# Two stacks of gated layers on one core: the order of work at the edges of the stages, and the token sums moved from GpSimd to VectorE

## The reference

```python
for l in range(2):                                   # first block
    x = x + 0.5 * swiglu(rmsnorm(x, ffn1_norm[l]), gate, up, down)    # ffn1_l
    h = rmsnorm(x, mix_norm[l])                                       # mix_l
    x = x + concat(sliding_window, moba, top_k_sparse)(h @ w_in[l]) @ w_out[l]
    x = x + 0.5 * swiglu(rmsnorm(x, ffn2_norm[l]), gate, up, down)    # ffn2_l
x = rmsnorm(x, final_norm)                                            # final
h = h + rms_norm(diff_attention(rms_norm(h)))        # second block: diff
h = h + rms_norm(conv_ffn(rms_norm(h)))              # conv_0
h = h + rms_norm(forgetting_attention(rms_norm(h)))  # fox
h = h + rms_norm(conv_ffn(rms_norm(h)))              # conv_1
```

## Time and profile before

| | us |
|---|---|
| median of 3 runs | 3137.25 (3136.92 to 3137.4) |
| the profiled execution | 3136.89 |
| its span in the trace | 3135.1 |
| PE busy | 3085.1 (98%) |
| DVE busy | 2095.1 (67%) |
| ACT busy | 1372.0 (44%) |
| POOL busy | 821.9 (26%) |
| granted clock of PE, mean | 0.998 of full speed |

### The profile page before, as it was taken

The page is one execution under the profiler, slowest core; times in us unless marked ns, Lnnn a source line. Parts: engine busy times, 40 slices in busy tenths (PEclk is TensorE's granted clock), DMA queues, the critical chain, the costliest instruction groups (busy, mean ns, idle before and its releaser), DMA issues.

```text
span 3135.1 us, 47847 instructions
## 1 busy us (share of the span) xinstructions
PE 3085.1 (98%) x17664; PEld 2608.0 (83%) x17664; DVE 2095.1 (67%) x3335; ACT 1372.0 (44%) x2308; POOL 821.9 (26%) x627
## 2 busy tenths in 40 slices
PE   8999999999999999999999999999999999999999
PEld 6999876898989899777899977677888886778887
DVE  6869587685958586695867753556556546576474
ACT  5535246452535353354634433644334335343242
POOL 3212346521333133264412220240000332310003
PEclk9999999999999999999999999999999999999999
DMA  4355331333334433221343333123333231223232
GB/s 125 106 148 153 102 101 41 94 102 101 104 85 115 114 88 102 77 61 54 101 121 89 103 93 96 39 61 87 107 87 100 81 96 41 68 68 109 86 99 82
DMA packets 530032, 289.14 MB, mean 92 GB/s; under 512 B 13630, under 2 KB 520225, under 8 KB 529850
## 3 DMA queue, kind: packets, MB, share of 16 engines
q1 hardware_dynamic: 527162, 281.26, 31.4%
q0 software_dynamic: 2688, 5.44, 0.5%
HBM read 284.38 MB, written 10.02 MB: 94 GB/s over the span
## 4 chain that ended last, share of the span: by engine, by line
PE 84%; DVE 7%; issue 3%; ACT 3%; POOL 1%; SPq 1%; DMA 0%; DVEq 0%; ACTq 0%; POOLq 0%
PE bank L2373 38%; PE bank L2426 24%; PE bank L2391 5%; PE bank L2679 3%; PE bank L2789 2%; PE bank L2408 2%; PE bank L2476 2%; PE bank L2831 2%; PE bank L2854 1%; PE bank L2611 1%; PE bank L2517 1%; ACT w_hi L1009 1%; DVE w_lo L1612 1%; DVE h_lo L1642 1%; DVE scaled_g L1725 0%
## 5 line engine op out<-in xcount | busy, mean ns | idle before, releaser
L1009 ACT ACTIVATE w_hi<-w_raw 128x1024 fp32r<-128x1024 f32 (+1 forms) x319 | 367.6, 1152 | 1003.4 <-PE bank L2373 612.0
L1612 DVE TENSOR_TENSOR w_lo<-w_raw,w_hi 128x1024 fp32r<-128x1024 f32 (+2 forms) x287 | 420.1, 1464 | 254.8 <-ACT w_hi L1009 254.7
L2373 PE MATMUL bank<-h_hi,w_hi 128*128 128x512 f32 (+1 forms) x1204 | 476.7, 396 | 11.5 <-DVE h_lo L1642 4.5
L2373 PE MATMUL bank<-h_hi,w_lo 128*128 128x512 f32 (+1 forms) x1204 | 469.3, 390 | 0.0
L2373 PE MATMUL bank<-h_lo,w_hi 128*128 128x512 f32 (+1 forms) x1192 | 464.8, 390 | 0.0
L2426 PE MATMUL bank<-h_hi,ws 128*128 128x256 f32 x2432 | 452.7, 283 | 0.4 <-DVE ws L1796 0.4
L2426 PEld LDWEIGHTS bank<-h_hi,ws 128*128 128x128 f32 x2432 | 385.9, 192 | 1.4 <-DVE ws L1796 0.8
L2426 PE MATMUL bank<-h_lo,ws 128*128 128x256 f32 x1216 | 344.1, 283 | 0.0
L2426 PE MATMUL bank<-t_hi,ws 128*128 128x256 f32 x1824 | 341.1, 283 | 0.0
L2373 PE MATMUL bank<-act_hi,w_hi 128*128 128x512 f32 x836 | 325.3, 389 | 0.0
L2373 PE MATMUL bank<-act_hi,w_lo 128*128 128x512 f32 x836 | 325.2, 389 | 0.0
(11 more groups left out here) (390 smaller groups left out, 6245.6 us busy)
## 6 DMA issues: line engine op xcount, KB each, us to landing
w_raw<-in_ffn_w_down_dram SPq DMA_DIRECT2D x64, 704.0 KB, 4.7
w_raw<-in_ffn_w_in_dram SPq DMA_DIRECT2D x88, 512.0 KB, 3.8
raw_g<-in_ffn_w_gate_dram SPq DMA_DIRECT2D x76, 512.0 KB, 3.9
raw_u<-in_ffn_w_up_dram SPq DMA_DIRECT2D x67, 512.0 KB, 3.8
w_raw<-in_ffn_w_out_dram SPq DMA_DIRECT2D x32, 704.0 KB, 4.6
w_raw<-in_w_in_dram SPq DMA_DIRECT2D x34, 512.0 KB, 3.8
w_raw<-in_a_w_qkv_dram SPq DMA_DIRECT2D x24, 512.0 KB, 3.8
w_raw<-in_w_out_dram SPq DMA_DIRECT2D x16, 512.0 KB, 3.9
```

Source lines behind the costliest of these rows:

```text
L1009: nc.scalar.activation(split_home(c)[0][:, 0:nk, 0:cols], raw[c % 2][:, 0:nk, 0:cols], ACT.Copy).then_inc(hi_ready, 1)
L1612: nc.vector.tensor_tensor(w_low[:, 0:nk, 0:cols], raw[c % 2][:, 0:nk, 0:cols], w_high[:, 0:nk, 0:cols].bitcast(f32), ALU.subtract).then_in ...
L2373: mm = nc.tensor.matmul(result(c)[0:cols, :], w[:, k, 0:cols], x[k], start=(k == 0 and n == 0), stop=(k == nk - 1 and n == 2))
```

## The change

SP loads unit 3 and the first fast pair's up columns ahead of the four `lam_in` tables, and ACT makes `hi(3)` ahead of the first block of `full_input`. The four token sums are made by DVE (`token_sum(name, n)`): in the first gated stage around the first pairs' work, in the other three the first two before `invert` and the last two behind `lo(c + 3)`; POOL no longer makes them. In the first gated stage `gate_whole(1)` comes before `product_whole(0)`. `output_gemm` with a following stage makes the last `take` before `h_low` 5, 6 and 7. POOL's `pair_scale` makes the low part of the unit between the first phase's scaling and the second's. ACT's `finish` makes `hi(c + 2)` behind its loops. In the convolution stages `lead` is 3 for the first half, ACT's `hi(at + 2)` does not wait for the gate bank, and in the third pair DVE makes `lo(at + 2)` before it empties the gate bank.

```diff
--- before.py
+++ after.py
@@ -677,10 +677,8 @@
             def fast_ff(name, gate, up, down):
 
                 c = BASE[name]
-                for u in range(3 if c == 0 else 0, 2 * FAST_FROM[0]):
+                for u in range(4 if c == 0 else 0, 2 * FAST_FROM[0]):
                     load(c + u, (gate, up)[u % 2][:, :, P * (u // 2):P * (u // 2 + 1)])
-                    if c == 0 and u == 3:
-                        fast_up(name, 0, FAST_FROM[0], up)
                 for j in range(FAST_FROM[0], FH):
                     fast_gate(name, 0, j, gate)
                     if c or j > FAST_FROM[0]:
@@ -745,6 +743,8 @@
                           A["attn_sinks"].rearrange("l h -> (l h)").partition_broadcast(P)).then_inc(small_in, 16)
             sp.dma_start(bf_col[FG_ROW:FG_ROW + 16, :],
                           A["b_f_2"].rearrange("(h a) -> h a", a=1)).then_inc(small_in, 16)
+            load(3, kview(A["ffn1_w_up"], 0)[:, :, P:2 * P])
+            fast_up(stages[0], 0, FAST_FROM[0], kview(A["ffn1_w_up"], 0))
             for n, w in enumerate(("a_lam_q1_2", "a_lam_k1_2", "a_lam_q2_2", "a_lam_k2_2")):
                 sp.dma_start(lam_in[:, n, :],
                               A[w].rearrange("l d -> (l d)").partition_broadcast(P)).then_inc(small_in, 16)
@@ -826,17 +826,6 @@
                     pool.dma_start(brow_one[r].ap(), brow[8 * r:8 * r + 8, :]).then_inc(tab_one, 16)
                 pool.wait_ge(tab_one, 16 * 3)
 
-            def token_sums(name):
-
-                t1, t2, at = HALF[0], HALF[1], 4 * FAST[name]
-                pool.wait_ge(full_ready, KT * FAST[name] + KT)
-                nc.gpsimd.tensor_tensor(t_raw[:, 0, :, :], h_full[:, 0:KH, t2], h_full[:, 0:KH, t1], ALU.subtract).then_inc(t_made, 1)
-                pool.wait_ge(t_made, at + 1)
-                nc.gpsimd.tensor_tensor(t_raw[:, 1, :, :], h_full[:, KH:KT, t2], t_raw[:, 0, :, :], ALU.subtract).then_inc(t_made, 1)
-                nc.gpsimd.tensor_tensor(t_raw[:, 2, :, :], h_full[:, KH:KT, t2], h_full[:, 0:KH, t2], ALU.subtract).then_inc(t_made, 1)
-                pool.wait_ge(t_made, at + 2)
-                nc.gpsimd.tensor_tensor(t_raw[:, 3, :, :], h_full[:, KH:KT, t1], t_raw[:, 1, :, :], ALU.subtract).then_inc(t_made, 1)
-
             def weight_sums(name, hf, j):
 
                 p, n = j % 2, of_pair(name, hf, j)
@@ -855,7 +844,6 @@
 
             def fast_ff(name):
 
-                token_sums(name)
                 for hf in range(HALVES):
                     rows = hf == 1 and name == stages[0]
                     if rows:
@@ -883,10 +871,12 @@
                                         sub_var[:, u, :].unsqueeze(2).broadcast_to([P, NT, P]),
                                         ALU.mult).then_inc(sub_diag, 1)
 
-            def pair_scale(stage, p):
+            def pair_scale(stage, p, unit=None):
 
                 plan = PLAN[stage, p]
                 for u, ph in enumerate(plan["used"]):
+                    if u == 1 and unit is not None:
+                        low(unit)
                     if ph not in plan["pool"]:
                         continue
                     pool.wait_ge(recip_ready, INVERTED[stage, p] + u + 1)
@@ -932,9 +922,8 @@
                     for i in range(POOL_LOW[0] + 1, MIX_Q + lead(name)):
                         low(BASE[name] + i)
                     for p in range(NP):
-                        if MIX_Q + p + lead(name) in POOL_LOW:
-                            low(BASE[name] + MIX_Q + p + lead(name))
-                        pair_scale(name, p)
+                        later = MIX_Q + p + lead(name)
+                        pair_scale(name, p, BASE[name] + later if later in POOL_LOW else None)
                 if name == "diff":
                     pool.wait_ge(tab_dram, 16 * 8 * 3)
                     if MIX:
@@ -1110,8 +1099,7 @@
                             part_copy(following, 0)
                         if half == 1 and k == 4:
                             half_root(following, 0)
-                        if half == 1 and k == 5:
-                            hi(c + 2)
+                hi(c + 2)
                 spread_copy(following, 0)
 
 
@@ -1141,7 +1129,7 @@
             def full_input(name):
 
                 for k in range(KT):
-                    if name == stages[0] and k == 2:
+                    if name == stages[0] and k == 0:
                         hi(3)
                     nc.scalar.activation(h_full[:, k, :], xres[:, k, :], ACT.Copy,
                                          scale=pre_gain(name, k)).then_inc(full_ready, 1)
@@ -1219,15 +1207,12 @@
                         else:
                             hi(c + 4)
                         product_high(0, 0)
+                        silu(0, 1)
+                        hi(c + 5)
+                        product_high(0, 1)
                         if early:
                             token_high(name, 1)
-                            hi(c + 5)
-                        silu(0, 1)
-                        if early:
                             token_high(name, 2)
-                        else:
-                            hi(c + 5)
-                        product_high(0, 1)
                     raw_high(hf, j0)
                     if hf == 0:
                         silu(0, 2)
@@ -1275,7 +1260,7 @@
                     c = BASE[name] + 30 * hf
                     cv = CV[name] + FH * hf
 
-                    lead = 2 if hf == 0 else 1
+                    lead = 3 if hf == 0 else 1
 
                     def pair(j, first=False):
                         at, jj = (c + 2 * j, 0) if isinstance(j, int) else (c + 2 * lead, j - lead)
@@ -1284,10 +1269,9 @@
                         made_g = (bank_free[c % 2], XT_USES + c // 2 + 1 + j)
                         made_v = (bank_free[(c + 1) % 2], XT_USES + (c + 1) // 2 + 1 + j)
                         early = at in FIRST
-                        if early:
-                            act.wait_ge(*made_g)
-                        else:
-                            hi(at + 2, jj, also=made_g)
+                        if not early:
+                            hi(at + 2, jj)
+                        act.wait_ge(*made_g)
                         if not first:
                             act_high(j - 1)
                         tap(tap_g, scaled_g, hf * FH + j)
@@ -1776,12 +1760,29 @@
                     return
                 lo(c + KT)
                 if follow:
-                    for k in range(KT - 1):
+                    for k in range(KT - 3):
                         h_low(follow, k)
                 take(c + KT - 1, KT - 1)
                 if follow:
-                    h_low(follow, KT - 1)
+                    for k in range(KT - 3, KT):
+                        h_low(follow, k)
                 lo(c + KT + 1)
+
+            def token_sum(name, n):
+
+                t1, t2, at = HALF[0], HALF[1], 4 * FAST[name]
+                if n == 0:
+                    dve.wait_ge(full_ready, KT * FAST[name] + KT)
+                    ins = nc.vector.tensor_tensor(t_raw[:, 0, :, :], h_full[:, 0:KH, t2], h_full[:, 0:KH, t1], ALU.subtract)
+                elif n == 1:
+                    dve.wait_ge(t_made, at + 1)
+                    ins = nc.vector.tensor_tensor(t_raw[:, 1, :, :], h_full[:, KH:KT, t2], t_raw[:, 0, :, :], ALU.subtract)
+                elif n == 2:
+                    ins = nc.vector.tensor_tensor(t_raw[:, 2, :, :], h_full[:, KH:KT, t2], h_full[:, 0:KH, t2], ALU.subtract)
+                else:
+                    dve.wait_ge(t_made, at + 2)
+                    ins = nc.vector.tensor_tensor(t_raw[:, 3, :, :], h_full[:, KH:KT, t1], t_raw[:, 1, :, :], ALU.subtract)
+                ins.then_inc(t_made, 1)
 
             def token_low(name, n):
 
@@ -1871,6 +1872,8 @@
                     c = BASE[name] + 2 * j
                     dve.wait_ge(silu_ready, FF[name] - CONV_FF[name] + 1 + j)
                     dve.wait_ge(mm_done, c + 2)
+                    if j:
+                        dve.wait_ge(act_ready, FF[name] + j)
                     nc.vector.tensor_tensor(prod[:, :], gated[:, :], result(c + 1)[:, :], ALU.mult).then_inc(bank_free[1], 1)
 
                 for hf in range(HALVES):
@@ -1881,18 +1884,24 @@
                         gate_whole(0)
                         if early:
                             lo(c + 4)
+                            gate_whole(1)
+                            token_sum(name, 0)
                         product_whole(0)
                         if not early:
                             lo(c + 4)
                         act_low(a0 + 1, 0)
-                        gate_whole(1)
+                        if not early:
+                            gate_whole(1)
+                            token_low(name, 0)
+                        product_whole(1)
+                        lo(c + 5)
                         if early:
-                            lo(c + 5)
-                        token_low(name, 0)
```

(23 more changed lines are left out.)

## The result

The changed kernel takes **3158.93 us** in the median of six runs (3156.43 to 3159.34), the kernel before 3137.18 (3136.11 to 3137.4): ratio 1.0068, 95% interval 1.0055 to 1.0081. It is slower by 21.8 us. The forecast was slower by 14.5, with a range that ended at 3158. The profiled execution, at 3156.43, was the fastest of the six; its span is 19.6 us above that of before.

What follows compares the result with a forecast made beforehand. PE was taken as the bound, busy 3085.1 of 3135.1 us. Start -0.6, mixing +12.3, edges +3.1, convolutions -0.4 gave +14.4 on 3136.89, 3151.3, and 3151.7 as median; range 3144 to 3158 (0.65).

Steps and rivals of the forecast that it cites:

- unit 73's low half: Mixing stage, pair 0: GpSimd scales first, so the low half ends at 458.67, PE wants it at 455.57; +3.1 us.
- pair 1: Mixing stage: PE's wait of 1.08 us for scalings behind the low half goes; -1.1 us.
- pair 4: Mixing stage, pair with three phases: the second phase's scalings end 2.1 us later, taken as +1.7 us.
- the clock: Lower granted clock behind the 3.1 us idle before unit 73; +1.5 us a mixing stage (0 to 1.5).
- the three gated stages: Edges into the later gated stages: unit c+4 waits for a later gate_whole(1); +0.6 us each, +1.8 together.
- The start: Unit 4's stall goes, first fast products 2.1 us sooner, but a new 3.3 us idle may lower the clock; -0.6 us.
- The mixing stages: GpSimd's new order: pairs sum to 4.65 us, clock 1.5, so 6.15 a stage and +12.3 for two.
- Pair 2: Mixing stage: GpSimd's new order costs +0.1 us here.
- Pair 5: Mixing stage: cost between 0 and +1 us, taken as 0.
- (3): Rival, slower still: VectorE bounds the gated stages, 1.5 us more in each of three, pair 5 1.0 twice; 3158.2, chance 0.12.
- the edges into the mixing stages: No token sum there; the lock between VectorE and GpSimd alone costs 0.8 us each (bound -1.0), +1.6 together.
- the convolution stages: Unit c+6: hi(c+6) 0.85 us sooner, but VectorE's low half precedes emptying c+4; gain 0.2 twice, -0.4 us.

Runs made afterwards that it cites:

- the second of experiment 1: Kernel before with only GpSimd's new order in the mixing stages (first phase's scaling ahead of the low half): 3157.99 us against 3137.34.
- that of 3: Changed kernel with the two loads (load 3, first pair's up columns) back behind the four lambda tables: 3158.9 us against 3158.93.
- the two of 4: Changed kernel with idle matmuls filling three pauses of PE: 24 a place 3160.42 us, 12 a place 3154.81, against 3158.93.
- Experiment 1: Changed kernel with GpSimd's old mixing order put back: 3139.55 us against 3158.93; kernel before with the new order alone: 3157.99 against 3137.34.

## Why the prediction was wrong in size and right in kind

**Right.** That the kernel becomes slower, and by which mechanism: unit 73's low half (3.1 forecast, 3.25 and 3.14 measured), pair 1 (-1.1; -1.25 and -1.26), pair 3 (+0.85; +0.87 and +0.87), pair 4 (+1.7; +1.72 and +1.78), the clock (+1.5; +1.58 in each stage, though in mix_1 behind pair 4 and not behind unit 73), the three gated stages (+0.6 each; +0.59, +0.67, +0.58), the diff edge (-0.3; -0.61). The lock between VectorE and GpSimd behaved as rows 9 let one expect: on the timelines of DVE and POOL after, three h_low take 3.88 us where three in a row take 2.0, and `psq` and `ssq` lie between them.

```profile
599.20 0.68 DVE L1737 TENSOR_TENSOR xres<-bank,xres 128x512 f32<-128x512 f32 x1
599.80 3.88 DVE L1626 SCALAR_TENSOR_TENSOR h_lo<-xres,gains,h_hi 128x512 fp32r<-128x512 f32 x3
...
600.02 1.42 POOL L815 TENSOR_TENSOR psq<-xres 128x512 f32<-128x512 f32 x1 [3.95 <-DVE xres L1737]
601.51 1.62 POOL L816 TENSOR_TENSOR ssq<-ssq,psq 128x512 f32<-128x512 f32 x1
```

**Wrong, by size.** Forecast and measurement lie 7.2 us apart in the medians and 5.1 in the profiled executions (14.4 against 19.5). Two terms were too small by 8.2 together, 3.4 at the start and 4.8 in the mixing stages; the others were too large by 3.1.

The start: -0.6 forecast, +2.8 measured. The step that failed is "it waits for almost nothing, even ahead of all eight h_full copies": I moved the load's arrival by as much as its issue, and left out that the eight copies then stand behind it. The issue itself moved by less than I took: four issues of 0.8 us would be 3.2, but in the trace before the four lambda issues and their gaps fill 2.38 us, and load 3 was issued 1.45 us sooner (23.67 for 25.12). Its hi(3) started 0.37 sooner, and two copies of 1.23 us together had moved behind it, which makes the 0.86. With `rstd` 0.86 later instead of 1.06 sooner, and lo(4) holding VectorE for 1.73 us instead of 1.13, `gate_whole(1)` ended at 42.68 instead of 40.15 and the VectorE chain at 57.67 instead of 55.3. From `gate_whole(1)` on the sum was right: 15.0 us measured, 15.15 forecast. The second half of that term, that the clock may fall behind the new pause, was priced at 1.5 and took 2.6, since the pause of 3.39 us was followed by 6 us at the lower clock.

The mixing stages: 6.15 forecast, 8.48 and 8.57 measured. Two pairs were undersized. Pair 2 was put at +0.1 and cost 0.75 and 0.89: its low half ends at 486.79 and PE begins at 486.84. Its reciprocal came 7.31 us later than before, while PE, by what pair 1 saved, lagged only 6.61, and the new order has no slack for the 0.7 between them. A saving in front of a resource that is next to bind is given back, and I had added the pairs as if they were independent.

Pair 5, taken at 0 of a range to 1, cost 1.53 and 1.55. It is not pair 4's case over again: the moved low half also holds up VectorE, a collision that the prediction priced at the start and at the edges but not here. `pen` is a short operation of VectorE that marks the largest scores of a later pair. The first row is from before, the others from after:

```profile
512.25 0.29 DVE L2016 TENSOR_SCALAR pen<-score 128x256 fp32r<-128x256 f32 x1
```

```profile
521.81 2.25 DVE L2028 TENSOR_SCALAR pen<-score 128x256 fp32r<-128x256 f32 x1
...
521.53 2.38 POOL L896 TENSOR_TENSOR w_lo<-w_raw,w_hi 128x1024 fp32r<-128x1024 f32 x1
...
524.93 5.42 POOL L889 TENSOR_SCALAR probs_mix<-probs_mix,recip 128x384 f32<-128x384 f32 x6 [1.02 <-DVE recip L2084]
```

`pen` starts inside GpSimd's low half and ends 0.15 behind it. The next `recip` stands behind `pen` on VectorE, so GpSimd, done with the low half at 523.91, stands idle for 1.02 us before it can scale, and PE waits 1.25 for the result. The same stands in mix_1 (2.24 us at 1439.40), and such a `pen` stands in both mixing stages of the four other kernels with this order for all pairs (the second of experiment 1, that of 3, the two of 4), and in none of the kernels without it. So 1.0 of the 1.5 is this collision; that it is the cause is read from the traces, and no run removes it alone. A low half is made in pair 6 as well, which the prediction left out; it cost nothing.

One of the rivals came close in number: (3), at 3158.2. It counted pair 5 at 1.0 a stage, which came true, and 1.5 more in each of three gated stages, which did not (+0.6 each, as forecast). So its number was near by luck.

Two smaller terms went the other way: the edges into the mixing stages, +0.8 each forecast, +0.4 each from just before to just behind the edge, where the last h_lo puts PE 0.7 back and the waits behind it return a part; and the convolution stages, -0.4 forecast and -2.3 measured, most of it not at unit c+6 (-0.53 and -0.54) but in small steps later, in the pairs of the loops. Whether those come from the lead or from the wait that hi(at + 2) lost was not tried apart.

That the median lies 2.5 us above the profiled execution was in no step. Experiment 1 fits: taking the order out gives 19.4 in medians, where the two stages' steps in the profile add up to 17.0. The clock's falls differ from execution to execution: the profile of the second kernel of experiment 1 has two in mix_1 where this one has one, at 1.6 us each. That this is the cause of the whole 2.5 is not shown.

## What to carry to other kernels

When a producer serves two consumers of one engine, the order of its two jobs is decided by which of them the consumer asks for first in each slot, not by a rule for all slots: here seven slots got one order, and one of them gained by it. Lay the producer's end time in the new order beside the consumer's demand time, slot by slot, and carry each slot's shift into the next. Ask also what the moved job now runs beside: here it blocked a third engine's short operation for 2 us. And a copy that fills another wait is not free to move behind that wait.

## What the runs showed of the hardware that was not expected

Behind its first matmuls the changed kernel has three pauses of PE of over 3 us. Behind the one of 3.39 the granted clock was 0.50 and 0.53 over the next 3 and 4 us, behind the one of 3.18 it was 0.66 over 4.2 us, and behind the third (unit 73 of mix_1, 3.07 us of idle) it was 1.00. It fell also behind shorter ones in some executions: in that of experiment 3 it was 0.50 over 3 us behind 1.96 us of idle, and 0.57 over 4 us behind 2.21. No single long pause is needed either. In pair 4 of mix_1, PE of the changed kernel stood still for 1.10 and for 1.25 us between matmuls, and then:

```profile
1425.00:1429.00 4.00, 1.65 (x8) 0.58 (x8) 3.32 (x11) 1.09 (x2) 4.00 (x6) 1.00 0.44 131
1429.00:1433.00 4.00, 4.00 (x12) 3.07 (x12) 2.28 (x8) 2.84 (x6) 1.69 (x2) 0.57 0.00 0
```

In pair 4 of mix_0, in the same execution, behind 1.05 and 1.25 us, the clock stayed at 1.00 (513 to 517). So none of these runs gives a length of pause that settles it. Independent of the change, some executions ran about 3 us of their first unit at the lower clock and others did not: the windows from 17 to 24 us of two kernels whose start is the same, before and the second of experiment 1:

```profile
17.00:20.00 3.00, 1.97 (x9) 1.66 (x10) 2.87 (x5) 3.00 (x6) 0.00 (x0) 1.00 0.71 201
20.00:24.00 4.00, 4.00 (x18) 3.05 (x17) 3.66 (x5) 4.00 (x7) 0.00 (x0) 1.00 0.09 30
```

```profile
17.00:20.00 3.00, 1.85 (x6) 1.52 (x7) 2.75 (x5) 3.00 (x6) 0.00 (x0) 0.80 0.67 192
20.00:24.00 4.00, 4.00 (x15) 3.17 (x14) 3.78 (x5) 4.00 (x7) 0.00 (x0) 0.72 0.14 42
```

Matmul number 48 starts 1.7 us later in the second, with one and the same work before it; PE's wait ahead of unit 4 takes it up (0.1 left there). The Trainium skill, "TensorE: Matmul & The Clock Gate", Part 1, says that the gate's phase is free-running, so that the same kernel sees its transitions at other places from run to run. The traces agree, with these 1.7 us. An idle matmul of 128 columns in fp32 cost 0.22 us, two records of 0.11 each.
